# Two-block sequence model on one core: the state stage's tables formed by POOL inside the attention stage, and the input products of all units placed ahead of the outputs

## The reference

```python
def s5_mixer(u, gate, lam_re, lam_im, log_step, b_re, b_im, c_re, c_im, d_skip, glu_w, glu_b, norm_w):
    # u: (1, 1024, 512) as 32 groups of 16 channels, each group with 64 complex states
    lr, li = minimum(lam_re, -1e-4), lam_im
    step = exp(log_step)[:, None]
    mag, ang = exp(lr * step), li * step
    ab_re, ab_im = mag * cos(ang), mag * sin(ang)
    den = lr * lr + li * li
    co_re = ((ab_re - 1) * lr + ab_im * li) / den
    co_im = (ab_im * lr - (ab_re - 1) * li) / den
    bb_re = co_re[..., None] * b_re - co_im[..., None] * b_im
    bb_im = co_re[..., None] * b_im + co_im[..., None] * b_re
    # state_t = ab * state_(t-1) + bb @ u_t (complex, per group), y_t = Re(c @ state_t) + d_skip * u_t
    y = gelu(y)
    val, gt = split(y @ glu_w + glu_b, 2)
    return rms_norm(val * sigmoid(gt) * silu(gate), norm_w)
```

## Time and profile before

| what | us |
|---|---|
| median of 3 runs | 3585.11 (3584.47 to 3597.44) |
| the profiled execution's own time | 3582.85 |
| its span | 3580.7 |
| attention, first DMA issue to the last store's issue | 947.5 to 1158.9 |
| first work of the next phase | 1161.96 |
| state stage, first DMA issue | 3135.28 |
| first issue of the last phase | 3356.66 |

### The profile page before, as it was taken

How to read it: one execution, slowest core, us unless ns; L and a number is a source line. 1 busy time by engine, 2 the same in 40 slices (tenths; PEclk the granted TensorE clock), 3 DMA queues, 4 the chain that set the end, 5 groups by cost and what they waited for, 6 DMA issues and landing times. The chain is left out here.

```text
span 3580.7 us, 53888 instructions
## 1 busy us (share of the span) xinstructions
PE 3004.7 (84%) x21257; PEld 2574.6 (72%) x21257; DVE 1949.6 (54%) x2543; ACT 1256.5 (35%) x1777; POOL 605.7 (17%) x299
## 2 busy tenths in 40 slices
PE   7999968888677599299999959699999886737699
PEld 6999957777544487288878847699999765634487
DVE  3365635666355333488888845310277674776421
ACT  2000004333254322277777734211111355422311
POOL 3223201111000000212222200122322221210000
PEclk9999988889788799599999979899999897967899
DMA  4565330000200732499999953424566612030421
GB/s 162 170 212 175 122 108 13 29 29 18 81 13 13 279 114 88 172 376 399 398 399 399 398 209 118 161 98 135 159 224 205 224 48 103 22 82 24 171 91 50
DMA packets 261101, 563.14 MB, mean 157 GB/s; under 512 B 31600, under 2 KB 105200, under 8 KB 259840
## 3 DMA queue, kind: packets, MB, share of 16 engines
q1 hardware_dynamic: 210672, 443.86, 34.9%
q10 hardware_dynamic: 40384, 82.65, 6.3%
q0 software_dynamic: 9872, 34.23, 2.6%
HBM read 437.66 MB, written 121.84 MB: 156 GB/s over the span
## 5 line engine op out<-in xcount | busy, mean ns | idle before, releaser
L360 PE MATMUL pin_psum<-pin_sb_w,pin_sb_hT 128*128 128x354 f32 (+1 forms) x5376 | 976.1, 344 | 25.9 <-DVE pin_sb_w L322 21.0
L360 PEld LDWEIGHTS pin_psum<-pin_sb_w,pin_sb_hT 128*128 128x128 f32 x5376 | 936.9, 189 | 62.0 <-DVE pin_sb_w L322 21.8
L4121 DVE TENSOR_TENSOR moe_sb_wlo<-moe_sb_raw,moe_sb_whi 128x2048 fp32r<-128x2048 f32 x192 | 438.1, 2288 | 94.6 <-ACT moe_sb_whi L3946 94.4
L3946 ACT ACTIVATE moe_sb_whi<-moe_sb_raw 128x2048 fp32r<-128x2048 f32 x192 | 367.4, 1916 | 137.1 <-DMA moe_sb_raw<-in_w_gate 50.0
L294 ACT ACTIVATE pin_sb_xt<-pin_psum,pin_sb_ss 128x353 f32<-128x353 f32 (+1 forms) x112 | 63.8, 589 | 564.8 <-PE pin_psum L360 515.9
L339 DVE TENSOR_SCALAR pin_sb_xt<-pin_psum,pin_sb_ss 128x353 f32<-128x353 f32 (+1 forms) x112 | 69.1, 625 | 330.6 <-PE pin_psum L360 330.4
L4189 PE MATMUL moe_psum<-moe_sb_whi,moe_sb_xhi 128*128 128x512 f32 x512 | 205.0, 400 | 16.2 <-DVE moe_sb_xlo L4125 16.2
L4189 PE MATMUL moe_psum<-moe_sb_wlo,moe_sb_xhi 128*128 128x512 f32 x512 | 201.7, 394 | 0.0
L4189 PE MATMUL moe_psum<-moe_sb_whi,moe_sb_xlo 128*128 128x512 f32 x512 | 201.5, 394 | 0.0
L253 POOL TENSOR_TENSOR pin_sb_w<-pin_sb_raw,pin_sb_w 128x2832 fp32r<-128x2832 f32 (+1 forms) x26 | 186.3, 7166 | 3.9 <-issue 0.6
L251 POOL CAST pin_sb_w<-pin_sb_raw 128x2832 fp32r<-128x2832 f32 (+1 forms) x26 | 76.2, 2931 | 642.4 <-PE pin_psum L360 596.2
(11 more groups left out here) (693 smaller groups left out, 5831.8 us busy)
## 6 DMA issues: line engine op xcount, KB each, us to landing
moe_sb_raw<-in_w_gate SPq DMA_DIRECT2D x64, 1024.0 KB, 12.4
moe_sb_raw<-in_w_up SPq DMA_DIRECT2D x64, 1024.0 KB, 14.0
moe_sb_raw<-in_w_down SPq DMA_DIRECT2D x64, 1024.0 KB, 12.6
pin_sb_raw<-in_w_in SPq DMA_DIRECT2D x16, 1412.0 KB, 7.5
scratch_proj<-pin_sb_xt ACTq DMA_DIRECT2D x16, 1412.0 KB, 6.3
pin_sb_raw<-in_w_in SPq DMA_DIRECT2D x12, 1792.0 KB, 8.7
scratch_proj<-pin_sb_xt ACTq DMA_DIRECT2D x12, 1792.0 KB, 6.3
scratch_ybuf<-moe_sb_yb ACTq DMA_DIRECT2D x32, 512.0 KB, 6.8
```

Of the source, the lines that this page charges most:

```text
L360: mm = te.matmul(ps[:, t, 0:cols], hT[a_part][:, k, t * P:(t + 1) * P], wt[b][w_part][:, k, :], start=(k == 0 and n == 0), stop=(k == KD - ...
L3946: s.activation(whi[q][:, :, :], raw[q][:, :, :], ACT.Copy).then_inc(hi, 1)
L4121: tt(wlo[q][:, :, :], raw[q][:, :, :], whi[q][:, :, :].bitcast(F32), ALU.subtract).then_inc(lo, 1)
```

## The change

A class `StateTables` holds the part of the tables that depends on weights alone. Its tiles are allocated in the attention phase, POOL computes them there with the same formulas, ScalarE does four exponentials/sines after its step 8 and its step 12, and VectorE one reciprocal in its step 12. Five results go to DRAM and are read back by `s5`.

```diff
+class StateTables:
+    OPEN, CLOSE = 8, 12
+    def scalar(self, s, i):                       # called after keep(i) on ACT
+        if i == self.OPEN:
+            s.wait_ge(self.prm_in, 96)
+            s.activation(C(3), C(2), ACT.Exp).then_inc(self.step_a, 1)
+        if i == self.CLOSE:
+            s.wait_ge(self.lr_p, 1)
+            s.activation(C(5), C(4), ACT.Exp)
+            s.activation(C(21), C(4), ACT.Exp, scale=float(SL)).then_inc(self.mag_a, 1)
+            s.wait_ge(self.ang_p, 1)
+            s.activation(C(8), C(6), ACT.Sin)
+            s.activation(C(9), C(7), ACT.Sin).then_inc(self.sin_a, 1)
+    def vector(self, v, i):                       # called after mix(i) on VectorE
+        if i == self.CLOSE:
+            v.wait_ge(self.norm_p, 1)
+            v.reciprocal(self.prm[:, 16, :], self.prm[:, 15, :]).then_inc(self.inv_d, 1)
+    def gpsimd(self, po):
+        # 6 DMAs of single elements (prm_in: lambda_re, lambda_im, log_step by halves), 2 of b (b_in)
+        # wait prm_in; C(10); wait step_a; 15 small instructions to ang_p, 3 more to norm_p
+        # wait sin_a, mag_a, inv_d; powers pw: 29 small instructions; pwr: 8 copies; wait b_in; bb: 6 of 256
+        self.keep(po, "pw", ...); self.keep(po, "bb", ...); self.keep(po, "mag", C(21))
+        # bls: 12 of 1024
+        self.keep(po, "bls", ...)
+        # sine and cosine doubling: 15 small; tab: 6 each of 16, 32, 64, 128, 256, 512, 1024 elements
+        self.keep(po, "tab", ...)
+        po.wait_ge(self.st, 80)

 def attention(nc, proj, col, out, g, tables):
+        @blk.gpsimd
+        def _(po):
+            po.wait_ge(x_in[NT - 1], 16)
+            po.wait_ge(v_in[NT - 1], 16)
+            tables.gpsimd(po)
```

In `s5` the VectorE and ACT instructions for these tables go, with the parameter rows and their transposes. The DMAs, the place of `kern` and the order of the engines change:

```diff
-        kern = zp[0:GH, :, :, :].rearrange("h k j c -> h (k j) c")
+        kern = uin[0:GH, :, :].rearrange("h s n -> h (s n)").rearrange("h (g c) -> h g c", c=P)
 SP:
+            sp.dma_start(ident[:, :], g["ident"]).then_inc(ident_in, 16)
+            # pw, bb, mag from DRAM -> pw_in (3 DMAs)
+            sp.wait_ge(c_in, 64)
+            sp.dma_start(uin[:, :, :], ...).then_inc(u_in, 16)          # was ACT's first instruction
+            sp.dma_start(flat, tables.out["bls"]).then_inc(bl_in, 16)   # 2 MB
+            sp.dma_start(tab[...], tables.out["tab"]).then_inc(tab_in, 16)   # 2 MB
             # then d, gluw, glub, nw as before
 ACT: cs copies (L3374) now ahead of the u copies (L3364); pwr copies gone; Silu of the gate after turn(0), turn(1)
 VectorE:
+            ve.wait_ge(pw_in, 48)            # then ca, as before
+            ve.wait_ge(tab_in, 16)
             ve.wait_ge(bl_t, 8)
-            ve.wait_ge(k_in, 16 * SL)
+            ve.wait_ge(u_t, 8)
-            for q in range(UNITS):
-                states(q)
-                if q:
-                    gelu_unit(q - 1)
-            gelu_unit(UNITS - 1)
+            for q in range(UNITS - 1):
+                states(q)
+            gelu_unit(0)
+            states(UNITS - 1)
+            for q in range(1, UNITS):
+                gelu_unit(q)
-            ve.wait_ge(gated_a, 2)           # now waited for per tile, before the gate's product
 TensorE: the 8 rounds of bls wait for bl_in; inputs(0), K, inputs(1) as before, then
-            for q in range(UNITS):
-                if q + 2 < UNITS:
-                    te.wait_ge(rotated, q + 1)
-                    inputs(q + 2)
-                te.wait_ge(k_in, 16 * SL)
-                outputs(q)
+            for q in range(2, UNITS):
+                te.wait_ge(rotated, q - 1)
+                inputs(q)
+            te.wait_ge(k_in, 16 * SL)
+            for q in range(UNITS):
+                outputs(q)
```

More of the change, by code:

```diff
@@ L2030, in rope_consts, with attention @@
     return np.concatenate([c, c, -s, s], axis=1).astype(np.float32)
-def attention(nc, proj, col, out, g):
+def attention(nc, proj, col, out, g, tables):
     with Phase(nc, "att") as ph:
@@ L2063, in attention @@
                                 "kept", "squared", "mean", "root", "normed", "passed"))
+        tables.open(ph)
         blk = ph.block()
@@ L2158, in _ @@
                 keep(i)
+                tables.scalar(s, i)
                 for at_step, tiles in BATCHES:
@@ L2230, in _ @@
                 mix(i)
+                tables.vector(ve, i)
                 if i + 1 < STEPS and not narrow(i + 1):
@@ L3306, in s5 @@
         blk = ph.block()
-        C = lambda i: prm[:, i, :]
         HALF = SL - 2
@@ L3375, in _ @@
             ins.then_inc(c_c, 1)
-            a.wait_ge(ang_d, 1)
-            a.activation(C(8), C(6), ACT.Sin)
-            a.activation(C(9), C(7), ACT.Sin).then_inc(sin_a, 1)
+            a.wait_ge(u_in, 16)
+            for i in range(4):
+                gs = slice(8 * i, 8 * i + 8)
+                a.activation(ug[:, gs, :].rearrange("p g (s h) -> p g s h", h=GH),
+                             uin[:, :, 128 * i:128 * i + 128].rearrange("p s (g h) -> p g s h", h=GH), ACT.Copy).then_inc(u_g, 1)
             for r in range(8):
@@ L3381, in _ @@
                 a.activation(uc[:, 4 * r:4 * r + 4, :], blocks(ps, r % 2, 4), ACT.Copy).then_inc(u_c, 1)
-            a.wait_ge(pw_d, 1)
-            for s in range(SL):
-                ins = a.activation(pwr[:, :, :, s], pw[:, :, :, SL - 1 - s], ACT.Copy)
-            ins.then_inc(pwr_a, 1)
             for r in range(8):
@@ L3411, in _ @@
                     gelu_out(n)
-            a.wait_ge(gate_in, 16)
-            for h in range(2):
-                a.activation(gate[:, 4 * h:4 * h + 4, :], gate[:, 4 * h:4 * h + 4, :], ACT.Silu).then_inc(gated_a, 1)
             def turn(t):
@@ L3422, in _ @@
             turn(0)
+            turn(1)
+            a.wait_ge(gate_in, 16)
+            for h in range(2):
+                a.activation(gate[:, 4 * h:4 * h + 4, :], gate[:, 4 * h:4 * h + 4, :], ACT.Silu).then_inc(gated_a, 1)
             for t in range(SL):
-                if t + 1 < SL:
+                if 1 <= t and t + 1 < SL:
                     turn(t + 1)
@@ L3529, in scaled @@
                 return s, p_, d, t
-            ve.wait_ge(pwr_a, 1)
-            for h in range(2):
-                s, p_, d, t = scaled(bls, bb, pwr, slice(8 * h, 8 * h + 8), SL)
-                tt(d[0], s[0], p_[0], ALU.mult)
-                tt(t[0], s[1], p_[1], ALU.mult)
-                tt(d[1], s[0], p_[1], ALU.mult)
-                tt(t[1], s[1], p_[0], ALU.mult)
-                ve.drain()
-                tt(d[0], d[0], t[0], ALU.subtract)
-                tt(d[1], d[1], t[1], ALU.add).then_inc(bl_d, 1)
-                ve.drain()
+            ve.wait_ge(pw_in, 48)
             ve.wait_ge(c_c, 1)
@@ L3675, in _ @@
         def _(te):
-            te.wait_ge(steps_set, 1)
-            for k in range(3):
-                mm = te.transpose(ps[:, 6, k * NJ:(k + 1) * NJ], nat[:, k, :], ident[0:NJ, 0:NJ])
-            mm.then_inc(prm_t, 1)
+            te.wait_ge(ident_in, 16)
             te.wait_ge(c_in, 64)
@@ L3692, in _ @@
                 mm.then_inc(u_t, 1)
-            for r in range(8):
-                h, i = r // 4, r % 4
-                k, j0 = i // 2, 8 * h + 4 * (i % 2)
-                te.wait_ge(bl_d, h + 1)
-                if r >= 2:
-                    te.wait_ge(bl_c, r - 1)
-                for i in range(4):
-                    mm = te.transpose(block_of(ps, 2 + r % 2, i), bls[:, k, j0 + i, :], ident[:, :])
-                mm.then_inc(bl_t, 1)
             def inputs(q):
@@ L3712, in inputs @@
                 mm.then_inc(b_mm, 1)
+            for r in range(8):
+                h, i = r // 4, r % 4
+                k, j0 = i // 2, 8 * h + 4 * (i % 2)
+                te.wait_ge(bl_in, 16)
+                if r >= 2:
+                    te.wait_ge(bl_c, r - 1)
+                for i in range(4):
+                    mm = te.transpose(block_of(ps, 2 + r % 2, i), bls[:, k, j0 + i, :], ident[:, :])
+                mm.then_inc(bl_t, 1)
             inputs(0)
             te.wait_ge(c_c, 1)
-            te.wait_ge(bb_d, 1)
+            te.wait_ge(pw_in, 48)
             for r in range(4):
@@ L4253, in build_program @@
     rwkv(nc, xs, o_rwkv, g["rwkv_masks"], g)
-    attention(nc, tokens, DIFF_IN, o_diff, g)
+    tables = StateTables(scratch("s5_bls", (P, 2 * NJ * P)), scratch("s5_tab", (P, 2 * NJ * SC)), scratch("s5_pw", (P, 2 * NJ * (SL + 1))),
+                         scratch("s5_bb", (P, 2 * NJ * GH)), scratch("s5_mag", (P, NJ)), g)
+    attention(nc, tokens, DIFF_IN, o_diff, g, tables)
     x1 = scratch("x1", (SEQ, D))
```

322 lines of the change are left out of this document (174 added, 148 removed).

## The result

| kernel | median us (runs) | ratio to before, 95% interval |
|---|---|---|
| before | 3587.07 (4) | |
| changed | 3546.36 (4) | 0.9882 [0.9866, 0.9898] |

What follows compares the result with a forecast made beforehand. Each phase has its own bound: tables on VectorE in the state stage, TensorE nearest in the attention. From 3582.85 profiled, -41 (state stage) and +20 (attention) give 3561.9; the median, 2.3 above, is 3564 us, range 3546 to 3588.

Steps and rivals of the forecast that it cites:

- bls rounds: State stage: eight rounds of ScalarE copies and TensorE transposes of bls, behind all of u's, take 8 us.
- K, copy, POOL, to the first DMA: State stage: K's 128 matmuls take 9.7 us, ScalarE's last copy 1, POOL's addition 1.4; then the kernel's DMAs start.
- the eight DMAs: State stage: the shifted kernel's DMAs still take 16.9 us, covered by VectorE's work but on the path to the first outputs.
- first output to last gelu: State stage: along VectorE's path through states(3) and gelu(1), then outputs(3) at the low clock; 39.6 us.
- the new order: State stage: states(3) and two units' outputs no longer follow one another; 10 of the 37.5 us gained by the last gelu.
- the port: Attention: VectorE stands at exposed instructions while POOL also reads; +13 us, bounds 2 and 40.
- Sines: Attention: ScalarE's sines for the tables cost 6 us, 3.4 and half a clock penalty; bounds 2 and 9.
- Loads: Attention: POOL's eight DMAs, six of single elements, run as a pipeline and cause no wait; other bound 30 us.
- My price for a norm step: Attention: forming bls beside a norm step costs VectorE 5 us, against 1.2 in each of three other steps.
- The slack hides the port: Rival, attention: VectorE's stands vanish in slack, so the attention costs 6 us and the time is 3550; chance 0.20.
- The low clock: Rival, attention: VectorE's stands make TensorE gaps, putting ten more steps at 1.2 GHz; time 3599 us, chance 0.12.
- Late data: Rival: single-element loads hold ScalarE in the attention, or u lands 12 us later in the state stage; 3576 us, chance 0.18.

Runs made afterwards that it cites:

- e1: Changed kernel with the state stage's new order undone, its tables still coming from the attention: 3572.92 us.
- e2: Kernel before with the state stage's new order alone, tables still formed in that stage: 3578.92 us.
- e4: Changed kernel without POOL's twelve instructions that form bls in the attention: 3546.92 us.
- e5: Changed kernel with both sines in the attention replaced by scaled copies that need no activation table: 3539.67 us.
- e6: Changed kernel with TensorE kept busy by transposes of the identity, 16 and 64, ahead of the state stage's outputs: 3543.20 us.
- e10: Changed kernel in which POOL forms bls twice in the attention, the second time right behind the first: 3565.67 us.

## Why the prediction was wrong, step by step

In the state stage the waits came in the order forecast, up to the first outputs, and sizes were off. Forecast and changed kernel, in us:

| step | forecast | measured |
|---|---|---|
| c landed, SP issues u (from the stage's start) | 7.7 | 6.2 |
| u landed, from its issue | 8.6 | 8.0 |
| ug and uc | 10.6 | 10.6 |
| bls rounds | 8 | 4.5 |
| input product of unit 0 | 2 | 1.9 |
| K, copy, POOL, to the first DMA | 12.1 | 9.9 |
| the eight DMAs | 16.9 | 14.7 |
| first output to last gelu | 39.6 | 40.3 |
| to the gated product | 1.7 | 1.8 |

**The first mis-sized term** is what stands in the middle, bls and K, where I took durations from rows with waits and a mixed clock in them. For bls's rounds I took 8 us from u's rounds (6.7), which run at a granted clock of 0.51 in the changed kernel; bls's own ran at 1.00 and took 4.5. K's 9.7 us were 3.7 for its first 64 matmuls (granted clock 1.00) and 6.0 for the other 64 (0.60), which stood 4.2 us for VectorE ahead of them. In the changed kernel nothing stands there, the granted clock is 1.00 from bls's rounds on, and all 128 take 7.2. Here the low clock behind the wait went with the wait; the forecast had the clock only as a bound in the other direction (K at the low clock, 4 us more). bls and K give 5.7 of the 9.4 us by which the last gelu came earlier than forecast; the eight DMAs give 2.2, c and u 2.1. The measured -50.7 lies outside my bound of -48. Why the DMAs were faster is open. K's new place in `uin` isn't the reason: from first issue to last landing they took 14.3 us in e1, with K in `zp`, and 16.1 in e2, with K in `uin`.

The row of 39.6 against 40.3 is right by luck. The forecast's path was VectorE's, with TensorE idle ahead of outputs(3). TensorE was never idle there: its four outputs of 9.2 us ran without a gap, and it reached outputs(3) 0.5 us after gelu(1) was done. VectorE's path, 27.2 us from the first output to gelu(1) where 26.9 were forecast, was just hidden by it. Where the outputs ran at a granted clock of 1.00 (e4 and e5 behind their first 4.6 us, e6), TensorE did idle 7.8 to 8.3 us ahead of outputs(3), as forecast.

The 10 us that I gave to the new order were those of the last third alone. e1 and e2 show that this split was wrong too: the order gives 8.6 us by itself and 23 beside early tables.

**The second mis-sized term** is what POOL's work costs VectorE in the attention, which the prediction calls the port, +13 of +20. Sines: forecast 6, measured 5.7 against e5, and 4.4 against the kernel before (21.1 less 16.7 from the mix of step 13 to that of step 16). Loads: the six of single elements were in 24.5 us behind the first issue, between my pipeline (14) and the serial bound (55), and ACT asked for them in the same microsecond; the largest wait seen in any profile is 0.8 us. The forecast had no wait, but its pipeline was 10 us too fast, so this was luck. Behind the mix of step 16, where POOL's long instructions run, the phase grew by 3.5 us in the first profile and by 6.9 as a mean of the six (against the mean of two of the old one); this stands against the 13. In the first profile its parts were, changed against before:

- from the mix of step 16 to that of step 19, under bls: 29.7 against 23.0, 6.7 more, where 8 were forecast; but by one stand of 6.0 us and five of 1.0 to 2.0, not by a norm step
- the steps to 20 and 21: 1.7 less, since the low clock that followed the square root's gap before isn't there (granted clock of the step to 20: 0.68 before, 1.00 here)
- from the mix of step 23 to that of step 31, under tab: 64.0 against 63.7, where 4 were forecast; the steps to 25 and 26 are 2.3 longer, those to 27, 28 and 31 give 2.0 back
- behind the mix of step 31: 1.7 less

My price for a norm step, 5 us, was near: in e4 and e10 a norm that was hit lasted 3.4 to 5.3 us longer, and its step 2.8 to 5.8 against the kernel before. That one would be hit was not: bls ended 1.9 us ahead of the first norm, and POOL then stood 6.6 us at its own store. I had counted no give-back at all. And the list of exposed lines was one short: the TENSOR_SCALAR of L2208 in the old kernel, of one SBUF tile, stood 1.0 us here and 7.8 in e5.

Two recorded sums are off by a little, and nothing measured hangs on them: three steps of 1.2 us and one of 5 are 8.6 and not 8, and 6 MB at the gate's rate for 2 are 24.9 us, so that u would have landed 16.6 and not 12 us later.

**The rivals.** "The slack hides the port" gave the attention 6 us and the time 3550; it is the nearest, and half right: two thirds of VectorE's 20 us vanished, but e10 shows that this isn't a property of the slack. The low clock came in part: in the steps to 15, 16, 17 and 18 the granted clock is 0.51, 0.54, 0.62 and 0.50 in the changed kernel, where it was 0.64, 0.83, 1.00 and 0.85 before. From the mix of step 19 to that of step 28 it is 1.00, even at the steps with 2.7 and 3.2 us at L2211, so the rival's ten slow steps weren't there. How much of the growth these four steps owe to the clock was tried for the sines alone. Late data did not come either.

**What was to show it.** L3743's successor at 55.7 us (66 forecast), last gelu 96.1 (105), u at 14.1 (16), attention 221.9 (235, and "under 8" more was named as wrong: met by the first profile's 7.5, not by the mean of 11), maxima at the counterpart of L2203 of 3.2 us (near 3, right), POOL's tab store 58 us ahead of the attention's last (right).

Behind one POOL instruction of 1.9 us the stands were 1.0 to 2.0 us. In the long ones, of 6.2 to 8.0 us, VectorE stood behind three or four POOL instructions in a row until a drain. These stands are what was measured: no run shows that the two engines share a port, or which of them gets in next.

## What to carry to other kernels

Work moved beside another stage costs what the instructions beneath it cost, and not its own length: taking 26 us of POOL's work out gained nothing here, since what followed moved to dearer steps, and adding 26 us cost 21. So list the exposed instructions step by step, and try drains between long ones. When a wait goes, don't take over a duration that was measured behind it: look at the granted clock that it was measured at. And an order of work may be worth little until what feeds it is early, so don't price the parts of such a change by one alone.
